# A hybrid SSD, RWKV-7 and mLSTM backbone step on one core: 80 products of constants on the matrix engine left out

## The chip, the core and the metric

The kernel runs on one core of a Trainium2 chip. The core has a matrix engine (PE, TensorE), whose weight loads are listed apart as PEld, a vector engine (DVE), a scalar engine (ACT), a third elementwise engine (POOL, GpSimd) and a queue engine (SP) that issues DMAs. PE works at one of two clocks, 2.4 GHz (granted clock 1.00) or 1.2 GHz (0.50), and the profile tells which was granted when. The metric is the time of one execution on the device in microseconds.

## The reference

One inference step of a trunk of two layers, with 128 context tokens and 512 latent tokens (640 columns in the kernel's layout), a model width of 1024 and everything in float32. Cut to what matters here:

```python
def _trunk_layer(x, mod, p, states, grid_w):
    sh1, sc1, g1, sh2, sc2, g2 = jnp.split(mod, 6, axis=-1)
    h = _rms_norm(x, p['norm1_g']) * (1 + sc1) + sh1
    u = h @ p['w_in']
    u_ssd, u_rwkv, u_ml = _split(u, [SSD_COLS, RWKV_COLS, MLSTM_COLS])
    ...
    y_ssd, n_ssd = _ssd_mixer(u_ssd, ...)     # chunked scan, both directions
    y_rwkv, n_rwkv = _rwkv_mixer(u_rwkv, ...) # low-rank decay and rate, then a scan
    y_ml, (n_c, n_n, n_m) = _mlstm_mixer(u_ml, ...)
    y = jnp.concatenate([y_ssd, y_rwkv, y_ml], axis=-1) @ p['w_out']
    x = x + g1 * y
    h = _rms_norm(x, p['norm2_g']) * (1 + sc2) + sh2
    x = x + g2 * ((jax.nn.silu(h @ p['ffn_w1']) * (h @ p['ffn_w3'])) @ p['ffn_w2'])
    return x, (n_ssd, n_rwkv, n_c, n_n, n_m)
```

The outputs are the tokens after both layers and a last normalisation, and the final states of the scans over the context.

## The kernel before, in words

The kernel is one program with a block of code per engine. Each block is an order written out by hand, and the blocks meet through semaphores: an engine waits until a named counter has reached a value (`pe.wait_ge(s["pair_read"], ...)`), and an instruction adds to a counter when it ends (`.then_inc`). No scheduler moves anything. In the names below, `at[...]` is the count that the layers before have used up.

A layer runs in this order on PE. First the input projection: 128 output columns at a time, for 640 tokens in two halves, with each float32 factor split into a high and a low part, so that three products (L1126 to L1128) take the place of one. Each tile of it is a pair of PSUM banks that ACT reads out (L2041, helper `pair_out`), and a count `pair_read` says that a pair is free again. The last pairs are the low-rank ones (`LORAS`, L1215): four groups of four products with 32 rows, two pairs of banks each. Groups one and two use four different pairs of banks; three and four use the same again, and so wait for `pair_read`.

Then the work is turned from features in partitions to tokens in partitions, in chunks of 128 tokens. For each of the five chunks `token_major` (L1264 to L1270) is a run of PE transposes, which ACT reads out (L2169 to L2173, count `ta_act`); `states_turned` (L1231 to L1249) turns the start states; `chunk_states` (L1285 to L1308) makes each chunk's own end state from operands that DVE (L2730, count `xe_ready`) and POOL (L881, count `ve_ready`) scale out of ACT's copies, and ACT reads it (L2162, L2163, count `cs_read`). PE does the transposes of chunk c + 1 ahead of the states of chunk c. On DVE longer work for the RWKV part (L2695, L2698) stands between the scalings.

Next come the weights and the y products of the SSD and mLSTM parts, again by chunk (`w_rows`, `y_ssd`, `y_mlstm`, `y_mlstm_state`, L1349 to L1434), where ACT takes exponentials, DVE multiplies and PE contracts in turn. At their end stands the entry of the RWKV part: PE transposes keys that POOL has made (L1489, L1491; POOL L945 to L952, count `rw_keys`), turns the last chunk's mLSTM output (L1445), makes the diagonal products (L1507, L1512), and sums squares with products of a single column (L1524), for which it waits for five sums of POOL (L973, count `ysq_sum`). The blocked inversion and the scan follow (L1537 onwards), then the output projection and the FFN, which are most of the kernel's time and are not touched.

A filler is a product whose result nobody reads: `warm(n, b)` (L1189 to L1193) multiplies the 128x128 identity in bfloat16 (`identb`) by the mask of constants `NEG`, 512 columns wide, n times into bank b. The bank is one that a later product with `start=True` overwrites. Calls of it stand ahead of the first low-rank group (4), between the groups (3 each), between the state transposes (2, twice), ahead of each chunk's states (2, five times), in the last chunk's mLSTM products (3), behind them (6), and ahead of the first diagonal products (4): 40 per layer, 80 in all. In `chunk_states` the filler stands between the waits for `ta_act` and `cs_read` and the wait for `xe_ready`.

Two other uses of the same constants stay: the masks that `w_rows` adds to its rows (L1353), which are part of the result, and zeros that it and `e_rows` add to the same banks (L1351, L1369).

Of the kernel before, what the change touches and what calls it, by code (L numbers as in the profile page):

```python
# [29 lines left out]
P = 128  # L30
# [113 lines left out]
def build(nc, io):  # L144

    with ExitStack() as ctx:
# [15 lines left out]
        PS = ctx.enter_context(nc.psum_tensor("PS", [P, 8, 512], F32))  # L162
# [29 lines left out]
        identb = ctx.enter_context(nc.sbuf_tensor("identb", [P, P], BF16))  # L192
        NEG = ctx.enter_context(nc.sbuf_tensor("NEG", [P, 2 * P], BF16))
# [81 lines left out]
        for d in range(2):  # L275
# [5 lines left out]
            b = {}  # L281
# [141 lines left out]
        for n, b in enumerate(BLOCKS):  # L423
# [11 lines left out]
            i = slot_of[n]  # L435
# [83 lines left out]
        with nc.Block() as block:  # L519
# [489 lines left out]
            def _(pe):  # L1009

                pe.wait_ge(setup["pool"], POOL_IDENT)
                n = 0
# [14 lines left out]
                mm, tr = nc.tensor.matmul, nc.tensor.transpose  # L1027
# [86 lines left out]
                for lay in range(DEPTH):  # L1114
# [44 lines left out]
                    for n in range(1, NU):  # L1159
# [3 lines left out]
                        if n > 1:  # L1163
                            w = split_block(n)
                            b = pair_banks()
# [5 lines left out]
                        for name, f in AFTER.get(n, []):  # L1171
                            b = pair_banks()
# [13 lines left out]
                            if u == UNITS - 1:  # L1186
                                picks.append(g)

                    def warm(n, b):  # L1189

                        for _ in range(n):
                            mm(PS[:, b, :], identb[:, :], NEG[:, :].unsqueeze(1).broadcast_to((P, 2, 2 * P)),  # L1192
                               start=True, stop=True)  # L1193


                    pe.wait_ge(s["lora_in"], at["lora_in"] + 48)
                    LAST_LORA = len(PAIRS) - len(LORAS)
                    assert pair[0] == LAST_LORA
                    warm(4, 0)
                    for i in range(0, len(LORAS), 2):  # L1200
                        n = LAST_LORA + i
                        if i < 4:
                            pe.wait_ge(s["pair_read"], at["pair_read"] + LAST_LORA)
                        else:
                            pe.wait_ge(s["pair_read"], at["pair_read"] + n - 2)
                        if i == 2:
                            pe.wait_ge(s["mod_ready"], 3 * lay + 3)
                        b = PAIR_BANK[n:n + 2]
                        if i:
                            warm(3, b[0])  # L1210
                        name, f = LORAS[i][0], LORAS[i][2]
                        for hf in range(2):
                            for d in range(2):
                                r = 32 * d + (0 if name == "w2" else 64)
                                ins = mm(PS[:, b[d] + hf, 0:HALF], lora[r:r + 32, f * P:(f + 1) * P],  # L1215
                                         tanx[r:r + 32, halves[hf]], start=True, stop=True)
                                if hf:
                                    ins.then_inc(s["pair_mm"], 1)
# [5 lines left out]
                    def states_turned():  # L1224
# [3 lines left out]
                        for d in range(2):  # L1228
                            for hh in range(SSD_H):
                                e, o = slice(64 * (hh // 4), 64 * (hh // 4) + 64), 256 * d + 64 * (hh % 4)  # L1230
                                mm(PS[e, 0, o:o + 64], SSI[0:64, 8 * d + hh, :], ident[0:64, 0:64], start=True, stop=True)  # L1231
                            warm(2, 2)
                            for f in range(2):
                                h2 = slice(4 * d + 2 * f, 4 * d + 2 * f + 2)
                                o = 128 * d + 64 * f
# [37 lines left out]
                    def chunk_states(c):  # L1273
# [3 lines left out]
                        if c:  # L1277
                            pe.wait_ge(s["cs_read"], at["cs_read"] + c)
                        dirs = [d for d in range(2) if (c < 4 if d == 0 else c > 1)]
                        warm(2, 4)  # L1280
                        pe.wait_ge(s["xe_ready"], at["xe_ready"] + c + 1)
                        if c == 0:
                            for d in range(2):
# [168 lines left out]
                    for c in range(NC):  # L1452
# [9 lines left out]
                        y_mlstm(c)  # L1462
                        if c < NC - 1:
                            w_rows(c + 1, 0, 2)
                        else:
                            warm(3, 2)
                        y_mlstm_state(c)
                        if c < NC - 1:
                            w_rows(c + 1, 1)
                            qk_products(c + 1)  # L1470
                            w_rows(c + 1, 2)
                    warm(6, 2)

                    def cpos(k, d):
                        return 0 if k == 0 else (k if d == 0 else 5 - k)
# [4 lines left out]
                    for k in range(NC):  # L1480
# [12 lines left out]
                        for d in range(2):  # L1493
                            b, a, i = units[d], 4 * d, 2 * k + d
                            rk, wk = b["RK"][k % 2], b["wk"]
                            if i == 0:

                                mlstm_back(NC - 1)
                                warm(4, 2)
                                pe.wait_ge(s["yt_read"], at["yt_read"] + NC)  # L1500
                            pe.wait_ge(s["rw_feat"], at["rw_feat"] + i + 1)
                            if k:
# [1793 lines left out]
```

## Time and profile before

| | us |
|---|---|
| median of 3 runs | 2075.1 (2074.01 to 2076.66) |
| the profiled execution, its own time | 2066.84 |
| its span, first to last instruction | 2065.1 |
| PE busy | 1959.2 (95% of the span, 20520 products) |
| PE weight loads busy | 1818.9 (88%) |
| DVE busy | 1320.7 (64%) |
| ACT busy | 897.8 (43%) |
| POOL busy | 771.0 (37%) |
| mean granted clock of PE | 0.985 |

The span begins with the first instruction and ends with the last; the execution's own time has a little around it. A product's start is the surer figure, since the ends of products are modelled. In a timeline row the first number is the start in microseconds from the span's start, the second the length of the merged row, then engine, line of the kernel, operation, the tiles written and read, their shapes, and how many instructions were merged; a bracket tells how long the engine was idle before it and what ended the wait. A float32 product of the program can stand there as two records.

### The profile page before, as it was taken

To read this page: it belongs to the slowest core of one execution; us is meant where nothing else is said; L and a number is where in the kernel's file an instruction comes from. 1 tells how busy PE (TensorE), PEld (TensorE's weight loads), DVE (VectorE), ACT (ScalarE), POOL (GpSimd) and SP (SyncE) were. 2 spreads that over 40 slices of the span, in tenths; PEclk is the share of its full clock that TensorE was granted. 3 is DMA by queue.
4 is the path that set the end of the run, shared out by engine and by line. 5 is a ranking of instruction groups with operands and counts; after the bars stand their busy time and mean duration, and the time that the engine had idled before them with its cause. 6 is when DMAs were issued, how large, how long until landed. Compare 5 with 4: busy or idle time off the path is not lost.

```text
span 2065.1 us, 47813 instructions
## 1 busy us (share of the span) xinstructions
PE 1959.2 (95%) x20520; PEld 1818.9 (88%) x20520; DVE 1320.7 (64%) x2049; ACT 897.8 (43%) x1703; POOL 771.0 (37%) x603
## 2 busy tenths in 40 slices
PE   6999999898998999999989999889889999999998
PEld 6999955788898999999989998568879999999998
DVE  5755358668679888831248453776776998888111
ACT  5535554334354444521164374544344644445121
POOL 5332254435333334333323231732253243433331
PEclk8999999999999999999999999999999999999999
DMA  8554210010122223344336441000112223222221
GB/s 278 165 174 124 80 19 2 23 29 26 42 72 72 82 83 94 89 142 136 85 93 195 141 143 31 9 22 3 29 25 72 72 74 90 82 82 78 77 74 70
DMA packets 255272, 169.44 MB, mean 82 GB/s; under 512 B 23872, under 2 KB 228222, under 8 KB 255062
## 3 DMA queue, kind: packets, MB, share of 16 engines
q1 hardware_dynamic: 254835, 166.32, 27.0%
q8 instruction: 163, 2.67, 0.6%
q14 instruction: 47, 0.39, 0.1%
q10 hardware_dynamic: 227, 0.07, 0.0%
HBM read 162.21 MB, written 4.15 MB: 81 GB/s over the span
## 4 chain that ended last, share of the span: by engine, by line
PE 79%; DVE 12%; ACT 4%; issue 2%; SPq 1%; POOL 1%; DMA 0%; DVEq 0%; ACTq 0%; POOLq 0%
PE PS L1126 13%; PE PS L1127 12%; PE PS L1128 12%; PE PS L1821 7%; PE PS L1822 7%; PE PS L1823 7%; PE PS L1537 4%; PE PS L1084 2%; ACT arena L2192 1%; SPq L542 1%; DVE U_r L3212 1%; PE PS L1192 1%; PE PS L1564 1%; DVE U L2821 1%; PE PS L1659 1%
## 5 line engine op out<-in xcount | busy, mean ns | idle before, releaser
L781 POOL TENSOR_TENSOR ring_r<-ring,whi_r 128x1024 fp32r<-128x1024 f32 (+1 forms) x128 | 311.8, 2437 | 658.9 <-ACT whi_r L2018 658.9
L1126 PE MATMUL PS<-rwp_r,whi_r 128*128 128x320 f32 x1440 | 453.3, 315 | 11.0 <-DVE arena_r L2483 4.6
L1128 PE MATMUL PS<-rwp_r,ring_r 128*128 128x320 f32 x1440 | 445.7, 310 | 0.0
L1127 PE MATMUL PS<-U_r,whi_r 128*128 128x320 f32 (+1 forms) x1048 | 323.9, 309 | 0.0
L1126 PEld LDWEIGHTS PS<-rwp_r,whi_r 128*128 128x128 f32 x1440 | 271.0, 188 | 24.8 <-issue 17.8
L1127 PE MATMUL PS<-arena_r,whi_r 128*128 128x320 f32 (+1 forms) x904 | 280.1, 310 | 0.0
L1128 PEld LDWEIGHTS PS<-rwp_r,ring_r 128*128 128x128 f32 x1440 | 271.2, 188 | 0.0
L2018 ACT ACTIVATE whi_r<-ring 128x1024 fp32r<-128x1024 f32 (+1 forms) x128 | 131.2, 1028 | 291.3 <-PE PS L1128 291.2
L3043 DVE SCALAR_TENSOR_TENSOR x<-PS,MOD,x 128x128 f32<-128x128 f32 (+2 forms) x96 | 36.3, 433 | 259.0 <-PE PS L1128 259.0
L1127 PEld LDWEIGHTS PS<-U_r,whi_r 128*128 128x128 f32 x1048 | 196.8, 188 | 0.3
L1127 PEld LDWEIGHTS PS<-arena_r,whi_r 128*128 128x128 f32 x904 | 170.7, 189 | 0.2
L791 POOL TENSOR_TENSOR ring_r<-ring,whi_r 128x512 fp32r<-128x512 f32 x60 | 102.2, 1714 | 140.3 <-DVE arena L3145 62.9
L1537 PE MATMUL PS<-arena 64*64 64x64 f32 x3840 | 135.9, 222 | 16.6 <-DVE arena L2920 7.7
L1537 PEld LDWEIGHTS PS<-arena 64*64 64x64 f32 x3840 | 123.4, 137 | 28.5 <-issue 9.3
L2041 ACT ACTIVATE U<-PS 128x640 f32<-128x640 f32 x56 | 39.3, 702 | 163.5 <-PE PS L1128 163.5
L2237 ACT ACTIVATE arena<-PS 128x512 f32<-128x512 f32 (+1 forms) x100 | 55.4, 554 | 107.5 <-PE PS L1537 107.5
L1126 PE MATMUL PS<-U_r,whi_r 128*128 128x320 f32 x320 | 99.1, 310 | 0.0
L1128 PE MATMUL PS<-U_r,ring_r 128*128 128x320 f32 x320 | 98.9, 309 | 0.0
L1823 PE MATMUL PS<-arena_r 128*128 128x320 f32 x304 | 94.0, 309 | 0.0
L1823 PE MATMUL PS<-rwp_r,ring_r 128*128 128x320 f32 x304 | 93.9, 309 | 0.0
L2192 ACT ACTIVATE arena<-PS,arena 128x128 f32<-128x128 f32 x240 | 65.6, 389 | 58.5 <-PE PS L1353 58.5
L3152 DVE TENSOR_TENSOR arena_r<-arena,whi_r 128x512 fp32r<-128x512 f32 x72 | 82.1, 1155 | 0.0
(506 smaller groups left out, 4985.1 us busy)
## 6 DMA issues: line engine op xcount, KB each, us to landing
ring<-in_ffn_w SPq DMA_DIRECT2D x120, 512.0 KB, 3.8
rwp<-in_ada_w SPq DMA_DIRECT2D x64, 512.0 KB, 5.0
ring<-in_w_in SPq DMA_DIRECT2D x50, 512.0 KB, 5.1
U<-in_ada_w SPq DMA_DIRECT2D x16, 512.0 KB, 8.8
ring<-in_w_out SPq DMA_DIRECT2D x16, 512.0 KB, 4.0
arena<-in_ada_w SPq DMA_DIRECT2D x16, 512.0 KB, 4.7
ring<-in_ffn_w SPq DMA_DIRECT2D x16, 384.0 KB, 3.2
out<-arena SPq DMA_DIRECT2D x5, 512.0 KB, 2.9
```

The costliest lines, as they stand in the source:

```text
L781: g.tensor_tensor(rings_r[:, slot_of[n], 0:size(n), :], slot(n)[:, 0:size(n), :], whis[:, q % 2, 0:size(n), :].bitcast(F32), ALU.subtract) ...
L791: g.tensor_tensor(rings_r[:, slot_of[block], k0:k0 + 4, :], a, hi_slot(i, n).bitcast(F32), ALU.subtract).then_inc(s["split_lo"], 1)
L1126: mm(out, w[0][:, k, :], hi[:, cols], start=start, stop=False)
L1127: mm(out, w[0][:, k, :], lo[:, cols], start=False, stop=False)
L1128: return mm(out, w[1][:, k, :], hi[:, cols], start=False, stop=stop)
L1537: ins = mm(PS[t_, 4 * d + bank, col0 + 64 * hh:col0 + 64 * hh + 64], b[lhs][t_, hh, :], IDC[t_, :] if rhs is None else b[rhs][t_, hh, :], ...
L1821: mm(out, w[0][:, k, :], hi[:, k, :], start=start and k == 0, stop=False, skip_group_check=True)
L1822: mm(out, w[0][:, k, :], lo[:, k, :], start=False, stop=False, skip_group_check=True)
L1823: ins = mm(out, w[1][:, k, :], hi[:, k, :], start=False, stop=k == 3, skip_group_check=True)
L2018: A(whis[:, q % 2, 0:size(n), :], slot(n)[:, 0:size(n), :], ACT.Copy).then_inc(s["split_hi"], 1)
L2192: ins = A(W[:, i, q * P:(q + 1) * P], PS[:, ROW_BANK[(9 * c + i) % 3], q * P:(q + 1) * P], ACT.Exp, bias=COLS[:, c, 1, r + q:r + q + 1])
L3152: v.tensor_tensor(ST_LOW[o], ST_SUM[o], hi_slot(i, SUM_OP[n]).bitcast(F32), ALU.subtract).then_inc(s["st_lo"], 1)
```

## The change

The helper `warm` and all its calls go. No semaphore is counted by a filler, so no wait elsewhere changes; a wait that stood in front of a filler now stands in front of the next real product.

```diff
--- before.py
+++ after.py
@@ -1186,17 +1186,9 @@
                             if u == UNITS - 1:
                                 picks.append(g)
 
-                    def warm(n, b):
-
-                        for _ in range(n):
-                            mm(PS[:, b, :], identb[:, :], NEG[:, :].unsqueeze(1).broadcast_to((P, 2, 2 * P)),
-                               start=True, stop=True)
-
-
                     pe.wait_ge(s["lora_in"], at["lora_in"] + 48)
                     LAST_LORA = len(PAIRS) - len(LORAS)
                     assert pair[0] == LAST_LORA
-                    warm(4, 0)
                     for i in range(0, len(LORAS), 2):
                         n = LAST_LORA + i
                         if i < 4:
@@ -1206,8 +1198,6 @@
                         if i == 2:
                             pe.wait_ge(s["mod_ready"], 3 * lay + 3)
                         b = PAIR_BANK[n:n + 2]
-                        if i:
-                            warm(3, b[0])
                         name, f = LORAS[i][0], LORAS[i][2]
                         for hf in range(2):
                             for d in range(2):
@@ -1229,7 +1219,6 @@
                             for hh in range(SSD_H):
                                 e, o = slice(64 * (hh // 4), 64 * (hh // 4) + 64), 256 * d + 64 * (hh % 4)
                                 mm(PS[e, 0, o:o + 64], SSI[0:64, 8 * d + hh, :], ident[0:64, 0:64], start=True, stop=True)
-                            warm(2, 2)
                             for f in range(2):
                                 h2 = slice(4 * d + 2 * f, 4 * d + 2 * f + 2)
                                 o = 128 * d + 64 * f
@@ -1277,7 +1266,6 @@
                         if c:
                             pe.wait_ge(s["cs_read"], at["cs_read"] + c)
                         dirs = [d for d in range(2) if (c < 4 if d == 0 else c > 1)]
-                        warm(2, 4)
                         pe.wait_ge(s["xe_ready"], at["xe_ready"] + c + 1)
                         if c == 0:
                             for d in range(2):
@@ -1462,14 +1450,11 @@
                         y_mlstm(c)
                         if c < NC - 1:
                             w_rows(c + 1, 0, 2)
-                        else:
-                            warm(3, 2)
                         y_mlstm_state(c)
                         if c < NC - 1:
                             w_rows(c + 1, 1)
                             qk_products(c + 1)
                             w_rows(c + 1, 2)
-                    warm(6, 2)
 
                     def cpos(k, d):
                         return 0 if k == 0 else (k if d == 0 else 5 - k)
@@ -1496,7 +1481,6 @@
                             if i == 0:
 
                                 mlstm_back(NC - 1)
-                                warm(4, 2)
                                 pe.wait_ge(s["yt_read"], at["yt_read"] + NC)
                             pe.wait_ge(s["rw_feat"], at["rw_feat"] + i + 1)
                             if k:
```

How PE's order changes is shown at two places, as rows of instruction, tiles and the counts that are waited for. The first is the low-rank groups, where `PS` is PSUM, `lora` the small weights, `ident` the identity of the transposes. Before:

```order
L1192 MATMUL PS<-NEG,identb 128x512 [waits lora_in]
L1192 MATMUL PS<-NEG,identb 128x512 x3
L1215 MATMUL PS<-arena,lora 128x320 [waits pair_read]
L1215 MATMUL PS<-arena,lora 128x320 x3
L1192 MATMUL PS<-NEG,identb 128x512 [waits mod_ready,pair_read]
L1192 MATMUL PS<-NEG,identb 128x512 x2
L1215 MATMUL PS<-arena,lora 128x320 x4
L1192 MATMUL PS<-NEG,identb 128x512 [waits pair_read]
L1192 MATMUL PS<-NEG,identb 128x512 x2
```

and after, where L1215 has become L1205 and L1264 has become L1253:

```order
L1205 MATMUL PS<-arena,lora 128x320 [waits pair_read,lora_in]
L1205 MATMUL PS<-arena,lora 128x320 x3
L1205 MATMUL PS<-arena,lora 128x320 [waits mod_ready,pair_read]
L1205 MATMUL PS<-arena,lora 128x320 x3
L1205 MATMUL PS<-arena,lora 128x320 [waits pair_read]
L1205 MATMUL PS<-arena,lora 128x320 x3
L1205 MATMUL PS<-arena,lora 128x320 [waits pair_read]
```

The fillers are gone, and the waits that the first of a group carried stand on the low-rank products.

The second is the end of the y products and the entry of the RWKV part. Before:

```order
L1192 MATMUL PS<-NEG,identb 128x512 x6
L1489 MATMUL PS<-ident,arena 128x128 [waits rw_keys,ys_read]
L1489 MATMUL PS<-ident,arena 128x128 x3
L1491 MATMUL PS<-ident,U 128x128 x2
L1489 MATMUL PS<-ident,arena 128x128 [waits rw_keys]
L1489 MATMUL PS<-ident,arena 128x128 x3
L1491 MATMUL PS<-ident,U 128x128 x2
L1445 MATMUL PS<-ident,arena 128x128 [waits ym_ready]
L1445 MATMUL PS<-ident,arena 128x128
L1192 MATMUL PS<-NEG,identb 128x512 x4
L1507 MATMUL PS<-arena 64x64 [waits rw_feat,yt_read]
```

and after, from the last mLSTM state product (L1422, formerly L1434) on:

```order
L1422 MATMUL PS<-arena,lora 64x65 x7
L1474 MATMUL PS<-ident,arena 128x128 [waits rw_keys,ys_read]
L1474 MATMUL PS<-ident,arena 128x128 x3
L1476 MATMUL PS<-ident,U 128x128 x2
L1474 MATMUL PS<-ident,arena 128x128 [waits rw_keys]
L1474 MATMUL PS<-ident,arena 128x128 x3
L1476 MATMUL PS<-ident,U 128x128 x2
L1433 MATMUL PS<-ident,arena 128x128 [waits ym_ready]
L1433 MATMUL PS<-ident,arena 128x128
L1491 MATMUL PS<-arena 64x64 [waits rw_feat,yt_read]
L1491 MATMUL PS<-arena 64x64 x7
```

The wait for `rw_keys` now follows directly on the mLSTM state products, and the one for `rw_feat` and `yt_read` directly on the transposes.

## Rows read from the trace of the kernel before

**Rows 1.** Page, part 4: who holds the chain that ended last.
```profile
PE 79%; DVE 12%; ACT 4%; issue 2%; SPq 1%; POOL 1%; DMA 0%; DVEq 0%; ACTq 0%; POOLq 0%
```

**Rows 2.** One line of the kernel, L1192: count, ns min/median/max, first and last start.
```profile
L1192 PE MATMUL PS<-NEG,identb x80: 376/379/634, 257.3 to 1381.5; 128*128 128x512 bf16 x80
```

**Rows 3.** Stretches: their length, each engine's busy time and granted clock.
```profile
core 0: us, PE busy (x) PEld busy (x) DVE busy (x) ACT busy (x) POOL busy (x), PEclk, DMA share, GB/s
265.50:291.00 25.50, 23.68 (x274) 17.95 (x272) 14.60 (x20) 14.21 (x46) 11.15 (x11) 1.00 0.15 17
363.30:370.10 6.80, 4.97 (x33) 3.13 (x35) 4.99 (x9) 2.77 (x8) 6.80 (x10) 0.50 0.02 6
370.10:373.50 3.40, 3.29 (x82) 3.17 (x76) 3.37 (x8) 0.00 (x0) 2.64 (x4) 1.00 1.11 300
373.50:376.90 3.40, 3.40 (x64) 3.32 (x64) 1.50 (x4) 0.60 (x1) 1.88 (x3) 0.50 0.01 2
```

**Rows 4.** Timeline of PE and ACT at the low-rank pairs: start, length, line, tiles, count.
```profile
257.25 1.02 PE L1192 MATMUL PS<-NEG,identb 128*128 128x512 bf16 x4
...
258.21 1.35 PE L1215 MATMUL PS<-arena,lora 32*128 32x320 f32 x8
...
259.48 0.82 PE L1192 MATMUL PS<-NEG,identb 128*128 128x512 bf16 x3
...
260.24 1.34 PE L1215 MATMUL PS<-arena,lora 32*128 32x320 f32 x8
...
265.57 0.66 PE L1264 MATMUL PS<-ident,U 128*128 128x128 f32 x4
...
257.31 0.70 ACT L2041 ACTIVATE U<-PS 128x640 f32<-128x640 f32 x1 [6.69 <-PE PS L1128]
259.58 1.48 ACT L2041 ACTIVATE rwp<-PS,PC 128x640 f32<-128x640 f32 x2 [1.57 <-PE PS L1215]
```

**Rows 5.** Timeline of PE, DVE and ACT at chunks 1 to 4; in brackets idle time.
```profile
278.28 0.59 PE L1192 MATMUL PS<-NEG,identb 128*128 128x512 bf16 x2
278.80 0.65 PE L1302 MATMUL PS<-whi,arena 128*64 128x256 f32 x4
...
281.75 1.08 PE L1302 MATMUL PS<-arena 128*64 128x256 f32 x8
...
288.94 0.59 PE L1192 MATMUL PS<-NEG,identb 128*128 128x512 bf16 x2 [1.16 <-ACT arena L2163]
...
1301.35 0.59 PE L1192 MATMUL PS<-NEG,identb 128*128 128x512 bf16 x2 [0.33 <-ACT arena L2163]
...
279.53 1.72 DVE L2730 TENSOR_TENSOR arena<-ring,arena 128x512 f32<-128x512 f32 x2
...
286.09 1.72 DVE L2730 TENSOR_TENSOR arena<-ring,arena 128x512 f32<-128x512 f32 x2
...
288.50 0.30 ACT L2163 ACTIVATE arena<-PS 128x130 f32<-128x130 f32 x1
```

**Rows 6.** Timeline of PE and POOL at the RWKV entry, both layers.
```profile
362.97 0.81 PE L1489 MATMUL PS<-ident,arena 128*128 128x128 f32 x4 [2.21 <-POOL arena L946]
...
366.04 1.12 PE L1489 MATMUL PS<-ident,arena 128*128 128x128 f32 x4 [1.83 <-POOL arena L946]
...
367.80 1.91 PE L1192 MATMUL PS<-NEG,identb 128*128 128x512 bf16 x4
...
371.11 2.36 PE L1524 MATMUL PS<-ones,U 128*128 128x1 f32 x20
...
367.50 3.46 POOL L973 TENSOR_TENSOR U<-U 128x256 f32<-128x256 f32 x5
...
1383.95 2.39 PE L1524 MATMUL PS<-ones,U 128*128 128x1 f32 x20
...
1379.91 3.45 POOL L973 TENSOR_TENSOR U<-U 128x256 f32<-128x256 f32 x5
```

**Rows 7.** Weight loads of one line that ran at both levels of the clock.
```profile
L1071 PEld LDWEIGHTS PS<-ident,NRC x20: 185/333/333, 29.2 to 1049.6; 128*128 128x128 f32 x20
```

## The prediction

> **What bounds the kernel now.** I read the page first. Its chain of work that ended last lies on the matrix engine (PE) for 79% of the span [rows 1], so a product taken off PE counts unless another engine is late right behind it. The second view is the one line of the fillers: 80 products of 512 columns, 379 ns each by the median, of which the first starts at 257.3 us and the last at 1381.5 [rows 2]. They are 40 per layer and stand in two places: 27 between the end of the input projection and the first y products (A), 13 at the entry of the RWKV part (B). The third view is the table of stretches with the granted clock: A runs wholly at 1.00 (2.4 GHz), and B holds two drops to 0.50 (1.2 GHz) in spite of its fillers [rows 3]. The rest is the timeline of the two places. The reader is to look there for what is late once PE comes earlier, since each wait behind a filler is on ACT, DVE or POOL.
>
> **The change part by part.** Nothing is added or moved; no data and no semaphore hang on a filler, only the wait that the first of a group carried goes over to the real product behind it. Times are of layer 0; layer 1 repeats them 1013.25 us later.
>
> *A1, before and between the four low-rank pairs (4 + 3 x 3 fillers).* The first four take 257.25 to 258.21, 0.96 us [rows 4]. But the first product behind them needs the last tile of the projection out of its bank, and ACT reads that until 258.01 (257.31 + 0.70). A wait of PE for ACT ends about 0.14 us after the read (in [rows 5] the read ends at 288.50 + 0.30 = 288.80, and PE starts at 288.94). So PE starts at 258.15 and wins 0.06 of 0.96. Each three more take 0.76 (259.48 to 260.24). Without them a pair costs PE 1.27 (258.21 to 259.48), but ACT needs 1.48 to read a pair out, and pairs three and four reuse the banks of one and two: ACT becomes the bound of this piece. ACT starts 1.37 after PE's first product, at 259.52, and the transposes (L1264) wait for its third pair: 259.52 + 3 x 1.48 + 0.14 = 264.10, against 265.57. Gain 1.5 of 3.24; the fourth pair is read by 265.44, which the work behind the first transposes does not wait for, since these last until about 265.8.
>
> *A2, states and chunk 0 (2 + 2 + 2).* A pair costs 0.52 (278.28 to 278.80 [rows 5]). The transposes and copies that PE waits for here are read out by ACT and DVE with about 2 us to spare, so all three pairs count: 1.56. Shift so far 3.0.
>
> *A3, chunks 1 to 4 (2 each).* Chunk 1 wins its 0.52: 3.5. Chunk 2 (L1302 at 281.75) needs the DVE product L2730, done at 281.25 (279.53 + 1.72), which moves by 3.0 only, as its input is transposed ahead of chunk 1. It ends at 278.23, and PE may start at 278.37: shift 3.4, so PE waits where the fillers were. Chunk 3 wins 0.52 again, 3.9. Chunk 4 needs the DVE product of 286.09, which moves with the transposes behind chunk 2: 287.81 - 3.4 + 0.14 = 284.5. In layer 1 the fillers of chunk 4 start at 1301.35 and its products 0.52 later, which is 288.62 in layer 0's time: shift 4.1. In layer 0 they stand at 288.94 since that wait was 1.16 us instead of 0.33. I take the 0.8 us more as a chance event of that execution and leave it to the lower end. What follows (ACT's table load, the weights, the y products) hangs on chunk 4, and moves with it. **A: 6.9 us of fillers per layer (0.96 + 3 x 0.76 + 7 x 0.52), 4.1 us won.** Bounds for A: 6.9 if nothing became late, 0 if ACT and DVE took it all.
>
> *B, nine fillers at the end of the y products.* Behind them PE waits for POOL, 2.21 and then 1.83 us ([rows 6], 362.97 and 366.04), and POOL waits for a DVE chain that starts at the last y_ssd product. PE only waits longer: gain 0.
>
> *B, four fillers at 367.80.* They run at the low clock and take 1.91 us. PE wins up to that there, but the next piece, L1524, needs POOL's five sums, which end at 370.96 (367.50 + 3.46), and it starts at 371.11 now [rows 6]: gain 0.1. In layer 1 POOL is done at 1383.36 (1379.91 + 3.45) and L1524 starts at 1383.95, since PE was late: gain 0.5 (1383.95 less 1383.36 and the same 0.14). **B: 0.5 us over both layers.**
>
> *The clock.* This has no row for after, so it gets bounds. In the rows the clock is low in 363.3 to 370.1, behind PE's 2.21 us of waiting, and again in 373.5 to 376.9, behind a stretch full of L1524, products of a single column [rows 3]. Between them it is up, and directly before that the four fillers ran. Without them PE may stay low from 363 to 377 or 380. The price is read from rows at either level: a full weight load, which is nearly all of an L1524 product, takes 185 ns high and 333 low [rows 7], so L1524's 2.36 us would become 4.2, +1.9. Another 3.4 us low behind it would lose 0.4 of their length (four transposes take 0.66 high and 1.12 low, [rows 4, 6]), 1.4. That is 3 us per layer at the most, none if the clock rises as it does now. In A the clock stayed at 1.00 through transposes and small products with 0.5 us of fillers every 3 to 5 us, and a single short drop like that of 373.5 would cost 3.4 x 0.4 = 1.4. I take 1.6 over all of it, nearer to nothing than to the 6 of both layers, since the row nearest to the new A is the old one, at 1.00.
>
> The Trainium skill (TensorE: Matmul & The Clock Gate, "What's actually happening") says that the low clock is the default and that activity releases it. The trace agrees at 370.1, behind the four fillers; by this rule the whole entry of B would be low, and the sum would end at the 3 us per layer.
>
> **Sum.** 2 x 4.1 + 0.5 = 8.7 us off, less 1.6 for the clock: 7.1. The profiled execution took 2066.8 us (span 2065.1 and 1.7 around it) and would take 2059.7. The median of the runs is 2075.1, 0.4% above it; the edit is worth the same there: **2068.0 us**. This kernel's measurement tells a change from none from about 0.2%, 4.2 us.
>
> **The rivals.**
> - *R1, the low stretch at B grows in both layers.* For it: the order of events at 370.1 above. Against: POOL holds PE up here anyway, so that a part of the slower work would run in waiting time. Price 3 us per layer: 2075.1 - 8.7 + 6 = 2072.4.
> - *R2, the clock falls in A and stays down.* Place: 265 to 291, in both layers, where nearly all products are transposes and 64-column products. By the factor of the transposes, 1.7, 21 us of work per layer would grow by 15: 2075.1 - 8.7 + 30 = 2096. Each us at the low clock costs 0.4, so it turns the result slower once more than 21 us in all, some 11 per layer, run low. Against: the clock is 1.00 there, and the fillers are only seven pairs of 0.52 us in those 25.5. The Trainium skill (same page, "Part 4: PE-mode transpose") has a sentence that speaks for it: for transposes the high clock "doesn't engage", as they don't count as busy in the same way. The stretch of A is at 1.00 with fillers between; no row has it without.
> - *R3, the waits swallow it.* ACT (A1) and DVE (A3) are already late behind the fillers; if PE's remaining lead is lost at the y products, where DVE and ACT take turns on the chain, nothing is won: 2075. Against: those turns start at chunk 4's products, not at a time of their own.
> - That the fillers stay in some form (two L1351 products of zeros per chunk do) changes no term.
>
> **How the numbers follow.** Forecast 0.57 (2064 to 2071, the low end with the 0.8 us of layer 0 and no clock loss, and 2 us for the scatter of the median), R1 0.25 (2070 to 2075), R3 0.08, R2 0.10. The range 2064 to 2076 leaves out R2 and the tails. Faster by over 0.2% (below 2070.9): the forecast and a third of R1, 0.65. Slower by over 0.2%: R2, nearly all, 0.09. The same: 0.26.
>
> **What would show it.** In the profile after: the first low-rank product about 0.9 us after the projection's end, ACT reading the four pairs without a gap; a PE wait for DVE ahead of chunk 2; chunk 4 about 4.1 us nearer to the projection's end; L1489's wait for POOL longer by what the nine fillers took; L1524 starting right at POOL's end. Wrong would be: a clock under 1.00 in A (R2), L1524's piece longer than 2.4 us (R1), or a shift at chunk 4 that is gone by the last y product (R3).

## The result, and the profile after

The kernel without fillers is slower: a median of 2089.69 us (2087.23 to 2092.0, 4 runs) against 2074.56 us (2072.04 to 2076.66, 4 runs) for the kernel before, a ratio of 1.0068 (95% interval 1.0051 to 1.0085; the quotient of the two medians alone is 1.0073). The forecast was 2068.0 and its range ended at 2076. Only R2 was to end above it, and it had 0.10; R1, with 0.25, was put at 2070 to 2075. The profiled execution took 2089.68 us (span 2088.0). Two runs of the kernel before among those beside e5 to e8, of 2414.24 and 3916.88 us, were slow ones and are left out of every median and ratio below.

The page of the kernel after, its busy times and its chain (answers to [rows 1]):

```profile
PE 1976.7 (95%) x20432; PEld 1847.5 (88%) x20440; DVE 1317.6 (63%) x2049; ACT 898.3 (43%) x1703; POOL 773.1 (37%) x603
...
PE 79%; DVE 11%; ACT 5%; issue 2%; POOL 1%; DMA 1%; SPq 0%; DVEq 0%; ACTq 0%; POOLq 0%
```

PE has 88 product records fewer (80 of them are the fillers) and is busy 17.5 us longer (1959.2 before). Fewer products that take more time are slower ones, so the clock is the next view. The kernel before first, by stretches of the two places, which I call A (from L1092, the first product behind the projection, to the last chunk's L1302) and B (from the last L1415 to the second run of L1537), in both layers; the columns are those of [rows 3]:

```profile
257.12:289.46 32.34, 31.18 (x309) 21.14 (x307) 15.10 (x23) 18.76 (x50) 10.73 (x11) 1.00 0.21 30
356.51:378.87 22.36, 18.12 (x256) 13.82 (x256) 17.08 (x37) 6.11 (x16) 14.70 (x18) 0.77 0.18 48
1270.36:1301.87 31.51, 31.18 (x309) 21.15 (x307) 14.26 (x23) 18.76 (x50) 10.71 (x11) 1.00 0.21 31
1368.94:1391.78 22.84, 18.33 (x256) 14.01 (x256) 17.06 (x37) 6.10 (x16) 14.68 (x18) 0.78 0.17 47
```

The same stretches of the kernel after, between the same products, with the low part inside each A and, in layer 1, the piece ahead of it:

```profile
260.51:296.46 35.95, 33.88 (x283) 26.62 (x281) 13.59 (x23) 18.64 (x50) 10.39 (x11) 0.72 0.19 27
272.20:292.70 20.50, 20.50 (x144) 16.82 (x140) 8.71 (x13) 7.98 (x28) 6.63 (x7) 0.50 0.16 20
365.58:390.07 24.49, 17.38 (x242) 15.49 (x242) 17.14 (x37) 6.22 (x16) 14.68 (x18) 0.65 0.16 44
1281.70:1320.62 38.92, 36.51 (x282) 28.91 (x281) 14.24 (x23) 18.86 (x50) 10.72 (x11) 0.65 0.17 25
1281.70:1285.90 4.20, 2.98 (x22) 2.12 (x22) 0.68 (x3) 2.50 (x4) 0.13 (x1) 1.00 0.73 124
1285.90:1313.20 27.30, 27.30 (x185) 22.09 (x183) 7.98 (x12) 11.51 (x31) 6.30 (x6) 0.50 0.13 16
1387.70:1413.12 25.42, 18.31 (x243) 16.17 (x243) 17.18 (x37) 6.22 (x16) 14.69 (x18) 0.60 0.15 43
```

A, which was wholly at 1.00, now runs 20.5 and 27.3 us at 0.50. PE does not wait in them: it is busy 20.50 of 20.50 us and 27.30 of 27.30. A is 3.6 and 7.4 us longer where the forecast had it 4.1 shorter. The clock did not fall at the same work in the two layers. In layer 0 it fell 11.7 us behind A's start, at the end of the state products. In layer 1 it fell 4.2 us behind it, in the low-rank products, of which 18 of 32 records had started. The first transposes of that layer start only at 1289.94.

PE and ACT of the kernel after at the low-rank groups and the first chunks (answers to [rows 4, 5]; L1205 is L1215 of before, L1253 is L1264, L1273 is L1285, L1290 is L1302, L2025 is L2041):

```profile
261.55 2.42 PE L1205 MATMUL PS<-arena,lora 32*128 32x320 f32 x16 [0.76 <-ACT U L2025]
264.43 2.71 PE L1205 MATMUL PS<-arena,lora 32*128 32x320 f32 x16 [0.46 <-ACT rwp L2025]
267.43 0.63 PE L1253 MATMUL PS<-ident,U 128*128 128x128 f32 x4 [0.29 <-ACT rwp L2025]
...
272.69 1.12 PE L1253 MATMUL PS<-ident,U 128*128 128x128 f32 x4
...
275.51 3.52 PE L1273 MATMUL PS<-arena 128*128 128x64 f32 x16
...
262.90 5.76 ACT L2025 ACTIVATE rwp<-PS,PC 128x640 f32<-128x640 f32 x8 [1.49 <-PE PS L1205]
```

ACT reads the four pairs in one piece, and PE waits for it, as forecast. Then, from 272.2 on, the same four transposes take 1.12 us instead of 0.63, with no wait ahead of them.

PE and POOL of the kernel after at B, both layers (answers to [rows 6]; L1474 is L1489, L1508 is L1524, L1521 is L1537):

```profile
372.05 1.09 PE L1474 MATMUL PS<-ident,arena 128*128 128x128 f32 x4 [4.37 <-POOL arena L946]
375.11 1.12 PE L1474 MATMUL PS<-ident,arena 128*128 128x128 f32 x4 [1.55 <-POOL arena L946]
380.17 4.40 PE L1508 MATMUL PS<-ones,U 128*128 128x1 f32 x20 [0.51 <-POOL U L973]
...
376.57 3.45 POOL L973 TENSOR_TENSOR U<-U 128x256 f32<-128x256 f32 x5
...
1402.28 4.40 PE L1508 MATMUL PS<-ones,U 128*128 128x1 f32 x20 [0.51 <-POOL U L973]
```

The wait for POOL took in the nine fillers (2.21 us before, 4.37 now), and L1508 starts at POOL's end (376.57 + 3.45 = 380.02, and 0.15). But it runs at the low clock in both layers, 4.40 us instead of 2.36 and 2.39.

Where the 22.9 us between the two spans lie, each the difference of a stretch between the same products in after and before:

| stretch | us | forecast |
|---|---|---|
| start to the end of layer 0's projection (260.51 - 257.12) | +3.4 | 0 |
| A, layer 0 | +3.6 | -4.1 |
| y products, layer 0 (69.12 - 67.05) | +2.1 | 0 |
| B, layer 0 | +2.1 | -0.1 |
| to layer 1's A | +0.1 | 0 |
| A, layer 1 | +7.4 | -4.1 |
| y products, layer 1 | 0.0 | 0 |
| B, layer 1 | +2.6 | -0.5 |
| the rest | +1.6 | 0 |

The first row is not the change's: nothing in front of it differs, and the profiles of all twelve kernels below reach that product 0.9 to 3.9 us later than the profile of before, whose execution (2066.84 us) lay 7.7 below the median of the four runs. In the y products of layer 0 the clock fell twice more, for 3.4 us each. The rows of A and B alone add up to 15.7 us, and the medians are 15.1 apart. The last row I have not traced. The clock allowance of 1.6 us over all has no row.

### The profile page after: what moved, and what is told of

Same layout as the page of the kernel before. It is cut to its first block, busy times and chain, and to the rows that moved or that the text cites. A ratio compares the mean times of both kernels' runs of the same rounds, so it can differ in the third digit from the quotient of the medians.

```text
span 2088.0 us, 47649 instructions
## 1 busy us (share of the span) xinstructions
PE 1976.7 (95%) x20432; PEld 1847.5 (88%) x20440; DVE 1317.6 (63%) x2049; ACT 898.3 (43%) x1703; POOL 773.1 (37%) x603
## 4 chain that ended last, share of the span: by engine, by line
PE 79%; DVE 11%; ACT 5%; issue 2%; POOL 1%; DMA 1%; SPq 0%; DVEq 0%; ACTq 0%; POOLq 0%
PE PS L1126 13%; PE PS L1128 12%; PE PS L1127 12%; PE PS L1805 7%; PE PS L1806 7%; PE PS L1807 7%; PE PS L1521 4%; PE PS L1084 2%; ACT arena L2176 1%; DVE U_r L3196 1%; PE PS L1548 1%; DVE U L2805 1%; PE PS L1643 1%; DMA U<-in_ada_w 1%; PE PS L1573 1%
## 5 line engine op out<-in xcount | busy, mean ns | idle before, releaser
L1126 PEld LDWEIGHTS PS<-rwp_r,whi_r 128*128 128x128 f32 x1440 | 272.2, 189 | 24.8 <-issue 17.8
L1521 PE MATMUL PS<-arena 64*64 64x64 f32 x3840 | 137.5, 224 | 18.4 <-DVE arena L2904 8.0
L791 POOL TENSOR_TENSOR ring_r<-ring,whi_r 128x512 fp32r<-128x512 f32 x60 | 102.0, 1711 | 140.7 <-DVE arena L3129 67.1
L1521 PEld LDWEIGHTS PS<-arena 64*64 64x64 f32 x3840 | 124.8, 138 | 30.3 <-issue 10.7
L2025 ACT ACTIVATE U<-PS 128x640 f32<-128x640 f32 x56 | 39.2, 701 | 174.0 <-PE PS L1128 173.9
```

The costliest lines, as they stand in the source:

```text
L791: g.tensor_tensor(rings_r[:, slot_of[block], k0:k0 + 4, :], a, hi_slot(i, n).bitcast(F32), ALU.subtract).then_inc(s["split_lo"], 1)
L1126: mm(out, w[0][:, k, :], hi[:, cols], start=start, stop=False)
L1521: ins = mm(PS[t_, 4 * d + bank, col0 + 64 * hh:col0 + 64 * hh + 64], b[lhs][t_, hh, :], IDC[t_, :] if rhs is None else b[rhs][t_, hh, :], ...
```

## The experiments

All are edits of the kernel before. Ratios are to runs of the kernel before on the same chip: medians 2073.74 us for e1 to e4 (20 runs), 2075.0 for e5 to e8 (18), 2072.86 for e9 to e12 (33). Lengths of A and B are between the same products as above. A time is the median of 4 to 12 runs, but a stretch is from one execution: that of e3 was the slowest of 5 (2096.36 us), of e9 the slowest of 8 (2090.07), of e2 and e4 the fastest of 4 and of 10 (2083.18 and 2075.45).

**Which place: e1 (B's fillers out, A's kept) and e2 (A's out, B's kept).**

```diff
 e1: warm(3, 2), warm(6, 2) and warm(4, 2) at B -> pass
 e2: warm(4, 0), warm(3, b[0]), warm(2, 2) and warm(2, 4) -> pass
```

> The 27 fillers per layer between the projection and the y products (place A) stay, the 13 at the RWKV entry (place B) go. Theory C (the clock): the profile after the change is at 0.50 for 20.5 and 27.3 us in A, and the RWKV entry costs 3 us more per layer there. With A's fillers back, A should be at 1.00 again and give back some 9 to 10 us; B should keep its longer low stretch: 2078 to 2081 us, against 2074.6 before and 2089.7 after. Rival W (the loss comes from the removed spacing of PE's products, whatever the clock): no stretch is special, the loss goes by the number of fillers, 13 of 40 gone: 2079.5 us, but with the shift spread evenly over A and B in the profile. Rival P (B's fillers are hidden behind POOL, as I predicted): 2074.6 us.

> The mirror: the 27 fillers of A go, the 13 of B stay. Theory C: A is low for about 20 us in each layer, B behaves as before: 2083 to 2086 us, and with e1 the two losses add up to the whole 15 us. Rival W: 27 of 40 gone, 2084.8 us, so this run does not tell C from W by time; C alone says that the granted clock is 0.50 in A and as before in B. If only both together keep the clock up, e1 and e2 will each stand near 2089.

e1: 2077.33 us, 1.0018 (1.0004 to 1.0032). e2: 2087.99 us, 1.0070 (1.0049 to 1.0091), as much as the kernel without any filler. Both lie outside what was expected, e1 0.7 us below and e2 2.0 above. Stretch B of e1 in layer 0, then A and B in layer 1:

```profile
362.37:387.75 25.38, 18.26 (x242) 16.12 (x242) 17.16 (x37) 6.22 (x16) 14.70 (x18) 0.60 0.16 43
1279.86:1312.92 33.06, 32.73 (x310) 22.24 (x308) 14.26 (x23) 18.76 (x50) 10.72 (x11) 0.95 0.20 30
1383.30:1405.64 22.34, 14.67 (x242) 12.82 (x242) 17.06 (x37) 6.10 (x16) 14.70 (x18) 0.77 0.17 48
```

R1 came true in one of two layers: 3.0 us longer in layer 0, and 0.5 shorter in layer 1. And A of layer 1, with all its 27 fillers, is at 0.95: the clock fell there 14.9 us behind A's start and was back after 3.4 us. So the fillers make a fall rarer and shorter, and do not rule it out. Stretches A of e2, and its products behind POOL's sums in layer 0:

```profile
261.06:297.07 36.01, 33.94 (x282) 26.69 (x281) 13.59 (x23) 18.64 (x50) 10.39 (x11) 0.72 0.19 27
...
1278.58:1318.38 39.80, 38.05 (x282) 29.79 (x281) 13.58 (x23) 18.86 (x50) 10.38 (x11) 0.61 0.16 24
```

```profile
380.73 2.36 PE L1524 MATMUL PS<-ones,U 128*128 128x1 f32 x20 [0.70 <-POOL U L973]
383.03 2.08 PE L1537 MATMUL PS<-arena 64*64 64x64 f32 x64
```

Leaving out A's fillers alone brings the whole low stretch. A second thing is to be seen: B of e2 took 20.82 us against 22.36 before. A drop of 3.4 us fell on 375 to 378, where the transposes end in a wait for POOL, and not on L1537, whose 64 products took 3.61 us before and 2.08 here. Here, then, what a drop cost hung on where it fell.

**Which fillers of A: e4 (only the 13 at the low-rank groups), e12 (the same, with B's) and e5 (only the 14 at states and chunks).**

```diff
 e4:  all but warm(4, 0) and warm(3, b[0]) -> pass
 e12: warm(2, 2) and warm(2, 4) -> pass
 e5:  all but warm(2, 2) and warm(2, 4) -> pass
```

> Of the 40 fillers only the 13 per layer ahead of and between the low-rank groups stay (A1). Theory C1 (the clock falls in the low-rank products, which use 32 rows, and A is low from there on because it cannot rise again): these 13 are enough for A, low stretch of A under 4 us, and the time is that of e1 less the 14 other fillers, 2074 to 2080 us. Theory C2 (the transposes and small state products fall by themselves): the clock still falls in A from 268 us on, 2084 to 2089 us.

> A1's 13 fillers per layer and B's 13 stay, the 14 of A2 and A3 go. e4 without B took 2079.5, and B is worth some 3.6 us (e1). If the two add up, 2075 to 2077 us: A2 and A3 are then worth nothing, what they take is what they give. If A2 and A3 are needed to hold the clock in the transposes, 2080 us or more.

> Only the 14 fillers per layer between the low-rank products and the y products stay (A2, A3: two per state group, two per chunk); the 13 ahead of and between the low-rank groups (A1) and the 13 of B go. e4 kept A1 alone and took 2079.5, e1 kept all of A and took 2077.3. Theory C1 (A1 is what keeps A up, because the clock falls in the low-rank products): A is low from 265 or 272 us on as in the kernel after, the 14 fillers run low too and end the low stretch sooner, after 7 to 14 us: 2083 to 2088 us. Theory C3 (either half will do): the clock stays up in A or falls for one piece of 3.4 us, 2076 to 2080 us, level with e4.

e4: 2079.49 us, 1.0030 (1.0016 to 1.0044). e12: 2075.84 us, 1.0015 (1.0000 to 1.0029). e5: 2094.05 us, 1.0101 (1.0077 to 1.0125), so it is, if anything, slower than with no fillers at all, and above what either theory gave it. e4 and e12 ended where C1 and the sum had them. Stretches A of e4, then of e12, then of e5, layers 0 and 1:

```profile
259.11:295.12 36.01, 35.47 (x295) 26.03 (x294) 13.59 (x23) 18.86 (x50) 10.39 (x11) 0.76 0.19 27
1278.19:1307.18 28.99, 28.02 (x296) 20.30 (x294) 13.71 (x23) 18.76 (x50) 9.46 (x11) 1.00 0.22 33
```

```profile
260.38:289.36 28.98, 28.02 (x296) 20.29 (x294) 13.70 (x23) 18.76 (x50) 9.46 (x11) 1.00 0.23 33
1274.52:1310.59 36.07, 35.53 (x296) 26.11 (x294) 13.60 (x23) 18.86 (x50) 10.40 (x11) 0.76 0.18 27
```

```profile
258.05:301.03 42.98, 41.44 (x297) 30.26 (x295) 14.26 (x23) 18.86 (x50) 10.72 (x11) 0.64 0.16 22
1281.86:1326.35 44.49, 41.47 (x296) 30.21 (x295) 13.65 (x23) 18.76 (x50) 10.45 (x11) 0.65 0.15 22
```

With the 13 alone A stays up in one layer and falls in the other, and which one differs between the two kernels although their A is the same code. So the same 29.0 us of products take 36.0 when the clock falls, here for 17 us; C1 had expected under 4. In e5 the clock fell 4 us behind A's start in both layers, in the low-rank products and ahead of the 14. It stayed low for 30.7 us, in layer 0 through 8 of the 14, and the fillers took 610 ns each by the median instead of 379: e5 pays for fillers and for the low clock both. But the 14 are not worthless inside a low stretch. In e1 the clock fell at the same place as in e4 and e12, 14 to 15 us behind A's start; with the 14 in place it was back after 3.4 us, in e4 and e12, without them, after 17. That is one fall against two, a hint and no proof.

**What in a filler counts: e3 (all 80 kept, 16 columns each), e10 (all 80 kept, 512 columns, with 32 columns of weights instead of 128), e9 (no fillers, but the low-rank products done twice).**

```diff
 e3:  mm(PS[:, b, 0:16], identb[:, :], NEG[:, 0:16], ...)
 e10: mm(PS[0:32, b, :], identb[:, 0:32], NEG..., ...)
 e9:  all warm(...) -> pass; for n_, hf in enumerate((0, 1, 0, 1)), counted at n_ == 3
```

> All 40 fillers per layer stay in number, place and waits, but each is 16 columns wide instead of 512. Theory C: what the fillers give is streamed columns; 16 are next to none, so the clock falls in A and at B as in the kernel after, 2088 to 2092 us. Rival W (order, waits, number of instructions, or the pause they make): the fillers are all there, so the time is that of before or, since each is shorter, up to 4 us under it, 2070 to 2075 us, and the clock stays up in A.

> All 40 fillers per layer stay, 512 columns of all 128 rows each, but with a stationary operand of 32 columns, so that they fill a quarter of the array. If the clock goes by time in which PE streams, nothing changes: 2072 to 2077 us. If it goes by how much of the array works, the fillers lose three quarters of their effect, the clock falls in A as in e3 (2089.7 us), and since these fillers still take their full time of 0.21 us and more each, 2090 to 2098 us.

> No fillers at all. Instead each low-rank group does its four products twice (the second time over the same bank, counted only then), so PE works without a pause in A1, as it did with fillers, but with products of 32 rows alone. Theory C1a (what the fillers gave in A1 is that PE had no pauses while it waits for ACT): the clock stays at 1.00 until the transposes, and A is low for less than in the kernel after: 2080 to 2087 us. Theory C1b (products of 32 rows are too little work for the clock, however dense): it falls in or right behind A1, A is low for 20 us and more in each layer, and the doubled products add 1 to 2 us per layer on top of the 2089.7 of the kernel after: 2090 to 2096 us.

e3: 2089.71 us, 1.0081 (1.0054 to 1.0108). e10: 2075.73 us, 1.0019 (1.0003 to 1.0036). e9: 2082.28 us, 1.0048 (1.0033 to 1.0064). The line of the fillers in e3 (count, ns min/median/max), and its stretches A:

```profile
L1192 PE MATMUL PS<-NEG,identb x80: 169/173/221, 260.6 to 1407.9; 128*128 128x16 bf16 x80
```

```profile
260.42:299.29 38.87, 37.91 (x310) 29.79 (x308) 13.50 (x23) 18.93 (x50) 10.29 (x11) 0.65 0.17 25
1285.29:1327.27 41.98, 41.02 (x310) 31.90 (x308) 13.50 (x23) 18.93 (x50) 10.30 (x11) 0.59 0.14 23
```

Stretches A of e10:

```profile
259.41:292.15 32.74, 31.85 (x309) 20.87 (x307) 14.93 (x23) 18.81 (x50) 10.73 (x11) 1.00 0.21 29
1276.09:1308.27 32.18, 31.86 (x310) 20.88 (x308) 14.37 (x23) 18.81 (x50) 10.73 (x11) 1.00 0.21 30
```

The same number of instructions at the same places did not hold the clock with 16 columns each, and with a quarter of the weights' columns they held it as with all. So neither the count of fillers nor the share of the array that they fill decided it here, but their width. One reservation: with the short fillers PE waits for ACT again ahead of the first low-rank product (0.57 us), so that e3 changes a wait there too. Over all of A it waits no longer than before, 0.96 us against 1.16. Stretches A of e9:

```profile
258.37:296.95 38.58, 37.28 (x315) 29.81 (x313) 13.59 (x23) 18.86 (x50) 10.39 (x11) 0.73 0.17 25
1285.12:1320.67 35.55, 34.25 (x314) 27.66 (x313) 13.59 (x23) 18.87 (x50) 10.38 (x11) 0.81 0.18 28
```

e9 gives PE real products in place of the 13 fillers ahead of the transposes, and behind one wait of 0.76 us they run for 8.5 us without a gap. The clock fell all the same, 14 and 15 us behind A's start, for 20.4 us in layer 0 and 13.7 in layer 1. So PE's waits for ACT in the low-rank groups are not needed for a fall. Whether the doubled products helped at all the times do not show, since the interval of e9 overlaps with that of the kernel after (1.0051 to 1.0085).

**How many: e7 (A's doubled), e11 (A's halved, 15 for 27), e6 (all halved, 22 for 40 per layer), e8 (20 more per layer at B).**

```diff
 e7:  warm(4, 0), warm(3, b[0]), warm(2, 2), warm(2, 4) -> 8, 6, 4, 4
 e11: the same four -> 2, 2, 1, 1
 e6:  as e11, and at B warm(3, 2), warm(6, 2), warm(4, 2) -> 2, 3, 2
 e8:  warm(6, 2) -> warm(14, 2), and warm(8, 2) behind the first keys' transposes
```

> The 27 fillers per layer of A become 54, B as before. The clock is up in A with 27 already, so this measures a filler's bare price: 0.25 us each on PE's path makes 6.9 us per layer, 2087 to 2089 us in all. If DVE and ACT hide a part of it as I reckoned for the way down (4.1 of 6.9 us), 2080 to 2083 us. If more fillers also raise the clock behind A (a y product stretch fell to 0.50 in some of the profiles), up to 2 us less.

> Half of the fillers in A (2 ahead of and between the low-rank groups, 1 in the states and in each chunk: 15 instead of 27), all 13 of B as before. In the profile of e6 A came out 3.1 and 1.6 us shorter with half its fillers, while B's half gave 1.6 us back in layer 0. So this should be the best of all: 2067 to 2072 us against some 2074.5, ratio 0.997 to 0.999. If e6's clock was chance, the same as before, 2074 us.

> Every call of the filler keeps about half of its products: 2 ahead of the low-rank groups, 2 between them, 1 in the states and in each chunk, then 2, 3 and 2 at B: 22 of 40 per layer. If the clock holds at 1.00 in A, the time saved by thinner fillers shows, some 2 us per layer: 2069 to 2073 us. If the clock's answer is one of all or nothing and half is too little, 2083 us or more. If it follows the amount evenly, 2080 to 2082 us (the middle of before and after).

> More fillers where PE only waits for POOL at the RWKV entry: 14 instead of 6 behind the y products and 8 more between the two groups of key transposes; they are 0.21 us each and should end before POOL does. The clock, at 0.50 from 363 to 370 and 374 to 377 us in the profile before, should be up in the first stretch: the products at 366 to 370 take half the time, but layer 0 waits for POOL's sums till 371 anyway. 1 to 3 us won over both layers: 2071 to 2073 us. If the clock there doesn't matter, 2074.

e7: 2089.91 us, 1.0075 (1.0053 to 1.0096). e11: 2068.62 us, 0.9982 (0.9968 to 0.9996; 12 runs). e6: 2071.17 us, 0.9998 (0.9981 to 1.0015). e8: 2077.92 us, 1.0013 (1.0000 to 1.0025), where 1 to 3 us were to be won. Stretches A of e7:

```profile
259.50:298.45 38.95, 37.01 (x336) 23.78 (x334) 15.27 (x23) 18.86 (x50) 10.72 (x11) 1.00 0.18 25
1286.10:1323.43 37.33, 37.00 (x336) 23.77 (x334) 15.12 (x23) 18.86 (x50) 10.72 (x11) 1.00 0.18 26
```

Stretches A of e11:

```profile
260.95:290.15 29.20, 28.65 (x298) 20.19 (x296) 13.99 (x23) 18.76 (x50) 10.14 (x11) 1.00 0.23 33
...
1278.30:1308.05 29.75, 28.66 (x298) 20.20 (x296) 14.55 (x23) 18.76 (x50) 10.24 (x11) 1.00 0.20 33
```

With the clock up in both, 27 fillers more cost 6.6 and 5.8 us per layer (38.95 - 32.34, 37.33 - 31.51), 0.25 and 0.22 each, and 12 fewer gain 3.1 and 1.8. e11 is the one kernel here that beats both, as was expected of it: its interval ends 0.04% below the kernel before, so it is faster by little, 3.7 us by the ratio. It is one of twelve kernels, though, and e6, with the same A (29.20 and 29.93 us at 1.00) and fewer fillers at B, is level with before. (Its profiled execution, 2074.73 us, was the slowest of its 12, for a reason that the section below has under R3.) PE of e8 at B of layer 0:

```profile
366.31 0.63 PE L1489 MATMUL PS<-ident,arena 128*128 128x128 f32 x4 [0.48 <-POOL arena L946]
...
374.44 2.36 PE L1526 MATMUL PS<-ones,U 128*128 128x1 f32 x20 [2.01 <-POOL U L973]
376.73 3.63 PE L1539 MATMUL PS<-arena 64*64 64x64 f32 x64
```

More fillers at B take away the drop of 363 to 370 and win nothing: the products with the clock up only wait longer for POOL's sums (L1526 starts 14.59 us behind the start of B, L1524 of before 14.60), and the short drop still falls on L1539. B is 22.37 us, as before.

**Where the clock fell in A.** Fourteen kernels with two layers each, from the granted clock in their profiles:

| fillers in A | fell, us behind A's start | low, us |
|---|---|---|
| none (after; e2) | 11.7 and 4.2; 11.5 and 4.4 | 20.5 and 27.3; 20.5 and 30.7 |
| 27 of 16 columns (e3) | 4.8 and 4.0 | 27.3 and 34.1 |
| the 14 at states and chunks (e5) | 3.9 and 4.1 | 30.7 and 30.7 |
| none, low-rank products twice (e9) | 14.3 and 14.9 | 20.4 and 13.7 |
| the 13 at the low-rank groups (e4; e12) | 14.4 and never; never and 14.7 | 17.0; 17.1 |
| all 27 (before, e1, e8, e10) | 14.9 in one of eight | 3.4 |
| 15 (e6, e11) or 54 (e7) | never in six | |

## Why the prediction was wrong

**The step that failed** is the paragraph "The clock". It allowed 1.6 us "over all of it, nearer to nothing than to the 6 of both layers, since the row nearest to the new A is the old one, at 1.00". That row holds the fillers whose removal was being priced, so it was no row for the kernel without them. What the runs showed in its place is a clock at 0.50 for 20.5 us of A in layer 0 and 27.3 in layer 1. The forecast arithmetic for everything else in A holds, and what the clock took can be worked out: A with the clock up and the 13 fillers is 28.98 (e12, layer 0) and 28.99 us (e4, layer 1); less the 1.5 that the 13 cost, 27.5 by estimate. After has 35.95 and 38.92, so 8.5 and 11.4 us were lost in 20.5 and 27.3 low ones, 0.41 and 0.42 per us, where the forecast had 1.6 for both layers and B together. R2 had that rate (0.4). Its price of 15 per layer was too high, since it had all 21 us of PE's work run low, and its place (265 to 291, at the transposes) was right in layer 0 only: in layer 1 the clock was down before them, in the low-rank products. R2 was right in its mechanism and given 0.10.

**The terms that held.**
- *A1, gain 1.5.* From A's start to the first transposes after takes 6.92 us (267.43 - 260.51) and before 8.45 (265.57 - 257.12): 1.53. ACT is the bound there, as forecast.
- *A2 and A3, 2.6 per layer, and 0.8 more in layer 0.* Shown where these fillers went and the clock stayed up: 3.36 in layer 0 (32.34 - 28.98, e12) and 2.52 in layer 1 (31.51 - 28.99, e4). The wait forecast ahead of chunk 2 is there in e12 (0.44 us at 283.15, though put down to ACT's L2169 and not to DVE). In after itself these terms cannot be seen.
- *B, nine fillers behind POOL: 0.* The wait grew from 2.21 to 4.37, and the start of L1524 behind the start of B did not move: 14.60 before and 14.59 after in layer 0.
- *B, four fillers: 0.1 and 0.5.* Measured 0.0 and 0.43 (15.01 to 14.58 in layer 1).

**R1 came true as well.** L1508 at the low clock is 4.40 us (estimate 4.2), and B grew by 2.1 and 2.6 us, the gain of layer 1 included, where R1 had 3.0 per layer. By itself this is no fixed price: of the ten stretches B without a filler, six are 24.1 to 25.4 us long (after and e9 in both layers, e1 and e4 in one) and four 22.3 to 22.4 (the other layers of e1 and e4, and both of e5):

```profile
368.06:390.40 22.34, 14.89 (x242) 13.12 (x242) 17.08 (x37) 6.22 (x16) 14.70 (x18) 0.77 0.17 48
...
1395.38:1417.74 22.36, 14.87 (x242) 13.10 (x242) 17.07 (x37) 6.16 (x16) 14.70 (x18) 0.77 0.17 48
```

In those four the clock fell and rose again much as before (0.77), with no filler in front of the rise. With fillers at B in place, on the other hand, B was 23.9 us twice (layer 0 of e10 with all 13 and of e6 with 7). So the order of events at 370.1 in before, clock up behind the four fillers, does not show that they raised it. I had made that argument for B, and had not asked at all what the fillers did in A.

**R3 holds in part.** It said that the y products would swallow A's gain by waits. Where A was shorter at 1.00 and no drop fell behind it, the y products took 0.5 us of the gain: in layer 1 of e4 the stretch from A's end to B's start is 67.57 us (1307.18 to 1374.75), before 67.07. In layer 0 of e12 it is 71.20 (289.36 to 360.56) against 67.05, and of e11 71.10, with the clock low at 296.0 to 299.4 and 296.6 to 300.1. PE of before and then of e12, the same products there:

```profile
295.21 1.09 PE L1386 MATMUL PS<-arena 128*64 128x128 f32 x16 [1.03 <-DVE arena L2748]
...
297.36 1.09 PE L1386 MATMUL PS<-arena 128*64 128x128 f32 x16
```

```profile
295.88 1.92 PE L1386 MATMUL PS<-arena 128*64 128x128 f32 x16 [1.03 <-DVE arena L2748]
...
299.62 1.09 PE L1386 MATMUL PS<-arena 128*64 128x128 f32 x16
```

The second run starts 2.15 us behind the first in before and 3.74 in e12. That is 1.6 of the 4.2 us; the rest is in single longer operations (L2705 on DVE 2.17 us against 1.48) and later starts that I have not followed up. The other profiles bear the drop out as the larger part: the six y stretches without a drop took 67.0 to 67.6 us (before twice, e4, e5, e8, e10). Of thirteen with a single drop 5.6 to 6.6 us behind A's end, eight took 70.4 to 71.2, all of them with 13 fillers or more in A, and five 67.1 to 67.8. So the gain can go behind A, but by another drop more than by the turns of DVE and ACT that R3 named, and fillers in A do not keep that drop away. The profiled execution of before had none, which fits its lying 7.7 us under the median.

**What the low clock went by.** The Trainium skill (TensorE: Matmul & The Clock Gate, "What's actually happening") has the low clock as the default that activity releases. The trace agrees in that A was low without the fillers and at 1.00 with them in seven of eight cases. It also shows that busy time as the profile counts it is not this activity: the clock was low with PE busy 20.50 of 20.50 us. The same page's "Part 4: PE-mode transpose" has it that transposes do not count as busy in the same way. The trace bears this out only in part. In layer 0 of after the clock was low through the transposes, but in layer 1 it fell ahead of the first of them; and A of e12's layer 0 has the same transposes with no filler between them and is at 1.00 throughout. So they do not force the low clock by themselves.

**What stays open.** Why A of after falls at different work in its two layers, why e4 and e12, the same code in A, fall in different layers, why e1 has R1 in one layer only, and why one drop behind A costs 3 to 4 us and another nothing. Whether these are settled by when A begins was not tried. The kernel before scatters by 13 us from run to run (2066.78 to 2079.95 in 33 runs), so single profiles of it differ by such events too.

## What to carry to other kernels

A product whose result nobody reads may be paying for the clock of the work behind it: before it goes, price the stretch around it at 1.2 GHz (here 0.4 us per us, on 20 us and more), and do not take the granted clock of a stretch that still has its fillers as evidence for the one without. Here fillers were worth having where PE is on the path and its own products are small (A, 1.0070 without them); where PE waits for another engine anyway they bought little (B, 1.0018). Those that stood ahead of the place where the clock falls counted most: without B's, the 13 early ones alone gave 1.0030 (e4), the 14 late ones alone 1.0101 (e5). Try half as many before none: here 15 of 27 held the clock in both layers of both profiles that have them, and e11 was the fastest kernel, by a small margin.

## What the runs showed of the hardware

- PE can be busy without a gap and stay at 1.2 GHz: 144 product records in 20.50 us, and 185 in 27.30 (after).
- The clock can fall in products of 32 rows and 320 columns, ahead of any transpose (after, layer 1, 4.2 us behind A's start; e5, both layers).
- 80 fillers of 16 columns (173 ns) left A at 0.65 and 0.59 (e3); 80 of 512 columns (379 ns) held it at 1.00 (before), and with a quarter of the weights' columns they held it too (e10, 1.00 and 1.00). With all 27 in A it still fell once in eight layers, for 3.4 us (e1, 0.95).
- Fillers in a stretch that was already low left it low for 30.7 us (e5) and took 610 ns instead of 379.
- At the low clock sixteen products of 64 columns took 3.52 us (after) against 1.89 to 1.90 at the high one (before, e12), and twenty single-column products 4.40 against 2.36; over a whole stretch the loss was 0.41 to 0.42 us per low us, by estimate.
